# One-core encoder kernel: loads reordered, condition pieces taken three chunks later, two chunks in banks of their own

## The chip, the cores and the metric

The kernel runs on one core of a Trainium2 chip. The metric is device time in microseconds (us) of one execution, the median of several runs. TensorE, VectorE, ScalarE and GpSimd are called PE, DVE, ACT and POOL in the rows; SP is SyncE, which issues every load.

## The reference

It is a chain of transformer blocks on one sequence of 512 positions and width 1024, all in float32. Cut to its steps:

```python
def first_block(x, mem, ...):
    proj = rms_norm(x, g) @ w_in                  # 1024 -> 3080: queries, keys, values, gates
    mix = concat(fox_attention, chunked_rel_attention) @ w_out
    x = x + rms_norm(mix)
    x = x + rms_norm(memory_cross_attention(...)) # w_mem_q, w_mem_kv, w_mem_o, 4 heads
    return x + rms_norm((silu(h @ gate) * (h @ up)) @ w_down)      # 1024 -> 2816 -> 1024

def second_block(x, c, ...):
    ada = silu(c) @ ada_w[l] + ada_b[l]           # 14 groups of 1024 numbers in all
    x = x + g1 * rmsnorm(mlstm_mixer(modulate(rmsnorm(x)), a_w_in, a_w_out))
    x = x + g2 * rmsnorm(square(relu(h @ w1)) @ w2)                # 1024 -> 4096 -> 1024
    ... # layer 2: latent attention (mla), then the same kind of MLP
```

## The kernel before

Everything lies transposed in SBUF: 8 blocks of 128 features by 512 positions. Each float32 product is made of three products of rounded halves: weight and input are split in a high part (rounded, fp32r) and a low part (the rest), and `three` (L774 to L778) issues high x high, high x low, low x high. PE works chunk by chunk: a chunk is 128 output features from one panel of weights (128x1024, 512 KB), 8 x 3 = 24 matmuls of 512 columns.

A panel passes four engines in order. SP loads it into `stage[:, slot]` (two slots, `load_panel`, L538), and may do so once the panel two before it is split (`s_split`). ACT copies it into its high part (`panel_high`, L1372), which it does in `used(p)` (L1390): it waits until PE has finished panel p, then waits for the landing of panel p+2, and copies that. POOL makes the low part (`split_low`, L656) and raises `s_split`, for which PE waits. The first four panels of a projection of the list JOINT have four pairs of weight buffers (EXTRA), so that ACT takes panels 4 and 5 already in `used(0)` and `used(1)`, and nothing in `used(2)` and `used(3)`.

Beside the panels the same SP queue loads 112 "condition pieces" (512 KB each, `load_piece`, L543), rows of the ada weights. Two slots again: piece q may be loaded once DVE has used piece q-2 (`s_pused`). DVE multiplies a piece by the condition vector and sums it into one column (`piece`, L2068). The queue is one list, in order: where SP waits for a piece's slot, the panels behind it wait too. The lists are written out by hand: `start_pieces`, `with_pieces`, `end_pieces` for w_in and a_in (panel, piece, piece, panel, ...), and L618 to L634 for the gated feed-forward.

In the projections w_in (16 chunks, then 8 value panels) and a_in (8 + 8 chunks, then 8 value panels) the chunks alternate between PSUM banks G[0] and G[1]; chunk c waits until DVE has taken chunk c-2 (`bank_free`). ACT's order for chunk c is: `used(c)`, that is the wait for panel c+2 and its copy, and then the copy of the result (L1451). DVE takes the low part of the result (`evacuate_low`, L2162) and then two pieces. After w_in's 16 chunks DVE waits for the gate logits, and ACT computes their logarithm after `used(16)` (L1468 to L1481).

The gated feed-forward has 11 groups of 6 panels: `up(g)` 4 panels (gate and up, twice), `down(g)` 2 panels. PE's order is up(0), up(1), down(0), up(2), down(1), up(3), ... With the panels counted from the stage's first, down(i) has panels 8+6i and 9+6i, up(i+2) has 10+6i to 13+6i. DVE takes four pieces after `add(g)`, the sum of down(g)'s eight results into Y. The two MLPs have the same form without a gate, with 2 + 2 panels per group and banks G[0] and G[1].

Other places of the change: the start (squares of x, their sum over partitions by PE, L883, the root, then the scaled input, L2006 and L2012), the self-attention's products with the values (`weigh`, L953, L979 to L982), the queries of the memory attention (mem_q), and the start of the latent attention (mla). `warm` (L865) issues matmuls whose result nobody reads.

## Time and profile before

| | us |
|---|---|
| median of 3 runs (2259.15 to 2264.13) | 2264.07 |
| the profiled execution | 2257.02 |
| its span | 2255.2 |
| PE busy | 2127.5 (94%) |
| DVE busy | 1087.3 (48%) |
| POOL busy | 958.2 (42%) |
| ACT busy | 876.0 (39%) |

PE is busy for 94% of the span. In the chain that ended last, 72% is PE and 13% "issue". Busy time says nothing of PE's clock: a matmul of 512 columns follows the one before it after 0.23 us at the full clock, and after 0.43 us where the granted clock is half. Rows of the timeline give start, duration, engine, line, operation, tiles, and in brackets the idle time before and what ended it. Rows of the windows view give for a stretch: its length, then busy us and count of PE, PEld, DVE, ACT, POOL, then the granted clock, the DMA share and GB/s.

### The profile page before, as it was taken

To read this page: it belongs to the slowest core of one execution; us is meant where nothing else is said; L and a number is where in the kernel's file an instruction comes from. 1 tells how busy PE (TensorE), PEld (TensorE's weight loads), DVE (VectorE), ACT (ScalarE), POOL (GpSimd) and SP (SyncE) were. 2 spreads that over 40 slices of the span, in tenths; PEclk is the share of its full clock that TensorE was granted. 3 is DMA by queue.
4 is the path that set the end of the run, shared out by engine and by line. 5 is a ranking of instruction groups with operands and counts; after the bars stand their busy time and mean duration, and the time that the engine had idled before them with its cause. 6 is when DMAs were issued, how large, how long until landed. Compare 5 with 4: busy or idle time off the path is not lost.

```text
span 2255.2 us, 27272 instructions
## 1 busy us (share of the span) xinstructions
PE 2127.5 (94%) x9534; PEld 1693.5 (75%) x9534; DVE 1087.3 (48%) x1672; ACT 876.0 (39%) x1442; POOL 958.2 (42%) x489
## 2 busy tenths in 40 slices
PE   5899889889999999889998999999999999999997
PEld 3777678677788888667766688888777776888886
DVE  2753661422465556655364543343565425343435
ACT  4224774344422222424265423222465544232332
POOL 2335676353344444423313344444435533444443
PEclk8999999999999999999999999999998999999999
DMA  4671034112254454347102223323222012233322
GB/s 172 211 266 45 20 116 146 57 37 75 66 179 159 156 171 164 112 159 262 65 1 69 67 84 95 101 93 95 91 78 72 1 47 66 88 98 93 100 95 84
DMA packets 66607, 234.38 MB, mean 104 GB/s; under 512 B 7136, under 2 KB 8416, under 8 KB 66400
## 3 DMA queue, kind: packets, MB, share of 16 engines
q1 hardware_dynamic: 66528, 233.33, 31.7%
q8 instruction: 49, 0.80, 0.1%
q14 instruction: 30, 0.25, 0.0%
HBM read 231.20 MB, written 2.10 MB: 103 GB/s over the span
## 4 chain that ended last, share of the span: by engine, by line
PE 72%; issue 13%; DVE 5%; ACT 5%; POOL 4%; DMA 1%; POOLq 0%; SPq 0%; DVEq 0%; ACTq 0%
PE bank L776 22%; PE bank L777 21%; PE bank L778 21%; POOL WL L658 3%; PE bank L883 2%; PE bank L868 1%; PE bank L950 1%; DVE H L2006 1%; DVE bank L2012 1%; PE bank L1017 1%; DVE Y L2248 0%; ACT Y L1556 0%; PE bank L889 0%; PE bank L1051 0%; PE bank L1276 0%
## 5 line engine op out<-in xcount | busy, mean ns | idle before, releaser
L658 POOL TENSOR_TENSOR WL<-stage,WH 128x1024 fp32r<-128x1024 f32 x272 | 660.6, 2429 | 1028.2 <-ACT WH L1378 1028.1
L1378 ACT ACTIVATE WH<-stage 128x1024 fp32r<-128x1024 f32 x272 | 288.2, 1060 | 918.6 <-PE bank L778 881.0
L776 PE MATMUL bank<-H,WH 128*128 128x512 f32 x1324 | 522.0, 394 | 25.3 <-DVE H L2006 11.8
L777 PE MATMUL bank<-H,WH 128*128 128x512 f32 x1324 | 519.4, 392 | 0.0
L778 PE MATMUL bank<-H,WL 128*128 128x512 f32 x1324 | 518.9, 392 | 0.0
L776 PEld LDWEIGHTS bank<-H,WH 128*128 128x128 f32 x1324 | 250.8, 189 | 84.9 <-issue 30.6
L778 PEld LDWEIGHTS bank<-H,WL 128*128 128x128 f32 x1324 | 250.8, 189 | 52.6
L777 PEld LDWEIGHTS bank<-H,WH 128*128 128x128 f32 x1324 | 250.9, 190 | 52.1 <-issue 0.5
L776 PE MATMUL bank<-HID,WH 128*128 128x512 f32 x688 | 268.8, 391 | 5.4 <-DVE Y L2248 5.4
L2248 DVE TENSOR_TENSOR Y<-bank,Y 128x512 f32<-128x512 f32 x344 | 226.3, 685 | 97.3 <-PE bank L778 96.4
L778 PE MATMUL bank<-HID,WL 128*128 128x512 f32 x688 | 268.4, 390 | 0.0
L777 PE MATMUL bank<-HID,WH 128*128 128x512 f32 x688 | 268.4, 390 | 0.0
L2071 DVE SCALAR_TENSOR_TENSOR apiece<-apiece,cond 128x1024 f32<-128x1024 f32 x112 | 184.9, 1665 | 106.9 <-DMA apiece<-ada 106.7
L2234 DVE SCALAR_TENSOR_TENSOR t<-bank,t 128x512 f32<-128x512 f32 x64 | 44.3, 692 | 276.5 <-ACT t L1599 276.4
L776 PEld LDWEIGHTS bank<-HID,WH 128*128 128x128 f32 x688 | 129.6, 188 | 32.5 <-issue 5.8
L2238 DVE TENSOR_TENSOR HID<-t,HID 128x512 fp32r<-128x512 f32 x86 | 121.3, 1411 | 65.0 <-ACT HID L1604 65.0
L777 PEld LDWEIGHTS bank<-HID,WH 128*128 128x128 f32 x688 | 129.7, 188 | 26.9
L778 PEld LDWEIGHTS bank<-HID,WL 128*128 128x128 f32 x688 | 129.5, 188 | 26.9
L868 PE MATMUL bank<-onesr,identr 128*128 128x512 f32 x284 | 81.8, 426 | 0.0
L690 POOL TENSOR_SCALAR sq<-sq,stat 128x256 f32<-128x256 f32 (+2 forms) x56 | 71.5, 1286 | 19.2 <-DVE stat L2183 19.1
L2177 DVE TENSOR_REDUCE stat<-bank 128x1 f32<-128x128 f32 (+3 forms) x112 | 53.3, 477 | 49.4 <-PE bank L1023 22.6
L1604 ACT ACTIVATE HID<-t 128x512 fp32r<-128x512 f32 x86 | 54.2, 631 | 56.3 <-DVE t L2234 50.6
(394 smaller groups left out, 3075.8 us busy)
## 6 DMA issues: line engine op xcount, KB each, us to landing
stage<-panels SPq DMA_DIRECT2D x296, 512.0 KB, 3.5
apiece<-ada SPq DMA_DIRECT2D x112, 512.0 KB, 4.3
RAW<-panels SPq DMA_DIRECT2D x18, 512.0 KB, 3.8
x<-xT SPq DMA_DIRECT2D x4, 1024.0 KB, 7.8
outT<-x SPq DMA_DIRECT2D x8, 256.0 KB, 2.0
Y<-bias SPq DMA_DIRECT2D x1, 1024.0 KB, 4.8
V<-memT SPq DMA_DIRECT2D x2, 512.0 KB, 4.5
con<-cons SPq DMA_DIRECT2D x1, 517.0 KB, 6.7
```

Of the source, the lines that this page charges most:

```text
L658: pool.tensor_tensor(low_of(p, slot), stage[:, slot, :], high_of(p, slot).bitcast(F32), ALU.subtract).then_inc(s_split, 1)
L690: pool.tensor_scalar(prob[b][:, 0:w], prob[b][:, 0:w], stat[:, 8 + b:9 + b], None, ALU.mult)\
L776: pe.matmul(out, wh, rh, start=start, stop=False)
L777: pe.matmul(out, wh, rl, start=False, stop=False)
L778: return pe.matmul(out, wl, rh, start=False, stop=stop)
L868: pe.matmul(out[:, :], identr[:, :], onesr[:, :].rearrange("p (a b) -> p a b", a=1).to_broadcast([P, 4, P]), start=True, stop=True)
L1378: act.activation(high_of(p, slot), stage[:, slot, :], ACT.Copy).then_inc(s_hisplit, 1)
L1604: act.activation(HID[:, slot, j, 0, :], t[:, j, :], ACT.Copy).then_inc(sm["high"], 1)
L2071: dve.scalar_tensor_tensor(apiece[:, k % 2, :], apiece[:, k % 2, :], 1.0, cond[:], ALU.mult, ALU.mult, accum_out=adac[:, column]).then_inc ...
L2177: dve.tensor_reduce(stat[:, b:b + 1], score_bank[b][:, 0:w], AX, ALU.max, negate=True)\
L2238: dve.tensor_tensor(HID[:, slot, j, 1, :], t[:, j, :], HID[:, slot, j, 0, :].bitcast(F32), ALU.subtract).then_inc(sm["split"], 1)
L2248: dve.tensor_tensor(Y[:, m, :], (T + O)[m % 4][:, :], Y[:, m, :], ALU.add)\
```

## The change

- w_in and a_in: the panels 4 and 5 are loaded ahead of the pieces 2 and 3; then a round of the list is piece, piece, panel, with panel 6 behind the pieces 2 and 3. DVE takes the first two pieces (0 and 1) after chunk 3 and so on, three chunks later than before; the rest follow after the last chunk (w_in: after the gates' first step).
- Chunks 2 and 3 of the JOINT projections go to the banks ST and AD, with no wait for a free bank. The MLPs use four banks in place of two.
- Gated feed-forward: pieces 40 to 43 are taken after `hidden(0)`, and each later four a group earlier. In SP's list the round of six panels with four pieces begins with panel 8 and piece 44, where it began with panel 12 and piece 42.
- Start: x is loaded in three parts, a small part of the constants (ident, ones) second, panels 0 and 1 ahead of the rest; PE waits for ones alone. ACT makes the extra panels after blocks 4 and 6 of the input. The condition's Silu moves behind chunk 0.
- mem_q: four panels are copied earlier, between squares and between blocks of the input.
- Self-attention: a pair's eight value products are spread over seven of eight steps; the results' copies and the values' staging move two steps later. mla: 12 `warm` matmuls ahead of it.

```diff
@@ -36,7 +36,11 @@
+PIECE_LAG = 3
+X_PARTS = [range(0, 2), range(2, 4), range(4, 8)]
+WEIGHED_AT = [[(0, 0), (0, 1)], [(1, 0), (1, 1)], [], [(0, 2)], [(1, 2)], [(0, 3)], [(1, 3)], []]
...
@@ -380,6 +384,10 @@
+        def own_bank(name, c):
+
+            return [ST, AD][c - 2] if name in JOINT and c in (2, 3) else G[c % 2]
...
@@ -530,10 +538,18 @@
         def _(sp):
-            sp.dma_start(x[:, 0:4, :], xT[0:4 * P, :].rearrange("(c p) t -> p c t", p=P)).then_inc(s_x, 16)
-            sp.dma_start(con[:], cons).then_inc(s_const, 16)
-            sp.dma_start(x[:, 4:8, :], xT[4 * P:8 * P, :].rearrange("(c p) t -> p c t", p=P)).then_inc(s_x2, 16)
+            for at, part in enumerate(X_PARTS):
+                sp.dma_start(x[:, part.start:part.stop, :],
+                             xT[part.start * P:part.stop * P, :].rearrange("(c p) t -> p c t", p=P))\
+                    .then_inc(s_x[at], 16)
+                if at == 0:
+                    sp.dma_start(con[:, 0:CON["mask"]], cons[:, 0:CON["mask"]]).then_inc(s_ones, 16)
             sp.dma_start(vec[:], vecs).then_inc(s_const, 16)
+            for slot in range(2):
+                sp.dma_start(stage[:, slot, :], panels[slot]).then_inc(s_stage[slot], 16)
...
@@ -545,29 +561,13 @@
-                        load_panel(i * 4 + (p0 + j), j % 2)
                         load_piece(i * 8 + (q0 + 2 * j), 0)
                         load_piece(i * 8 + (q0 + 2 * j + 1), 1)
-
-            def end_pieces(p0, q0, panels):
-
-                for j in range(max(panels, 3)):
-                    if j < panels:
-                        load_panel(p0 + j, j % 2)
-                    if j < 3:
-                        load_piece(q0 + 2 * j, 0)
-                        load_piece(q0 + 2 * j + 1, 1)
+                        load_panel(i * 4 + (p0 + j), j % 2)
 
@@ -578,13 +578,18 @@
 
-            sp.dma_start(cond[:], c).then_inc(s_c, 16)
-            sp.dma_start(wgate[:], gates_w).then_inc(s_gw, 16)
-            start_pieces(0, 0)
+            load_piece(0, 0, True)
+            load_piece(1, 1, True)
+            plain(2, 4)
             sp.wait_ge(s_h, row(MAKES, "x")[1])
             sp.dma_start(Y[:, 0:4, :].rearrange("p a b -> p (a b)"), bias).then_inc(s_bias, 16)
-            with_pieces(4, 2, 4)
-            end_pieces(20, 34, 6)
+            plain(4, 6)
+            pieces_ahead(6, 2, 4)
+            for j in range(4):
+                if j < 3:
+                    load_piece(34 + 2 * j, 0)
...
@@ -616,28 +621,31 @@
-            plain(p0, p0 + 12)
+            plain(p0, p0 + 4)
             load_piece(q0, 0)
             load_piece(q0 + 1, 1)
-            with sp.Fori(0, 4) as i:
-                for half in range(2):
-                    for j in range(6):
-                        load_panel(i * 12 + (p0 + 12 + 6 * half + j), j % 2)
-                        if j < 4:
-                            load_piece(i * 8 + (q0 + 2 + 4 * half + j), j % 2)
-            for j in range(6):
-                load_panel(p0 + 60 + j, j % 2)
-                if j < 4:
-                    load_piece(q0 + 34 + j, j % 2)
-            load_piece(q0 + 38, 0)
-            load_piece(q0 + 39, 1)
-            plain(p0 + 66, p0 + 68)
+            plain(p0 + 4, p0 + 8)
+            load_piece(q0 + 2, 0)
+            load_piece(q0 + 3, 1)
+            with sp.Fori(0, 9) as i:
+                for j in range(6):
+                    load_panel(i * 6 + (p0 + 8 + j), j % 2)
+                    if j < 4:
+                        load_piece(i * 4 + (q0 + 4 + j), j % 2)
+            plain(p0 + 62, p0 + 68)
             p0, q0 = PANEL0["a_in"], 80
             plain(p0 + 2, p0 + 4)
             load_piece(q0, 0)
             load_piece(q0 + 1, 1)
-            with_pieces(p0 + 4, q0 + 2, 3)
-            end_pieces(p0 + 16, q0 + 26, 8)
+            plain(p0 + 4, p0 + 6)
+            pieces_ahead(p0 + 6, q0 + 2, 3)
+            for k in range(26, 30):
+                load_piece(q0 + k, k % 2)
+            load_panel(p0 + 18, 0)
+            load_piece(q0 + 30, 0)
+            load_piece(q0 + 31, 1)
+            load_panel(p0 + 19, 1)
+            plain(p0 + 20, p0 + 24)
...
@@ -780,10 +788,14 @@
-                bank_free(pe, name, c)
+                if isinstance(c, int) and c in (2, 3) and name in JOINT:
+                    held = own_bank(name, c)
+                else:
+                    bank_free(pe, name, c)
...
@@ -976,10 +988,9 @@
                             score_pair(s + 4)
-                        if s >= 8 and s % 8 < 4:
-                            n, piece = 2 * (s // 8 - 1) + s % 2, s % 8 // 2 * 2
-                            weigh(n, piece)
-                            weigh(n, piece + 1)
+                        if s >= 8:
+                            for h, piece in WEIGHED_AT[s % 8]:
...
@@ -1066,8 +1076,10 @@
-                            if not (isinstance(g, int) and g == 0):
+                            if gated and not (isinstance(g, int) and g == 0):
                                 pe.wait_ge(sm["hidden"], g * 2 + j - 1)
+                            if not gated and not (isinstance(g, int) and g < 2):
...
@@ -1351,6 +1363,7 @@
+            warm(AD, 12)
...
@@ -1570,7 +1583,7 @@
-                        if s >= 12 and s % 8 in (4, 5):
+                        if s >= 12 and s % 8 in (6, 7):
...
@@ -1661,25 +1674,28 @@
-            squares("x", xc, lambda m: act.wait_ge(s_x if m < 4 else s_x2, 16))
+            squares("x", xc, lambda m: [act.wait_ge(s_x[at], 16) for at, part in enumerate(X_PARTS) if part.start == m])
             panel_high(0, 0)
             panel_high(1, 1)
             root("x")
+            act.wait_ge(s_ones, 16)
             act.wait_ge(s_const, 32)
-            extra_high("w_in", 0)
-            high("x", scaled_in, hh, lambda m: col("zero"))
-            extra_high("w_in", 1)
+            for m in range(KC):
+                high_chunk("x", m, scaled_in, hh, lambda m: col("zero"))
+                if m in (4, 6):
...
             def high_near(c):
 
+                if c == 0:
+                    act.wait_ge(s_c, 16)
...
@@ -1730,6 +1746,9 @@
+                if m in (1, 3):
+                    act.wait_ge(s_used, PANEL0["mem_v"] + m // 2 + 1)
+                    panel_high(RING1 + m // 2, m // 2)
...
-            panel_high(RING1, 0)
-            panel_high(RING1 + 1, 1)
             for m in range(KC):
                 high_chunk("x_mem", m, scaled_mem_in, hh, lambda m: col("zero"))
+                if m in (2, 5):
+                    act.wait_ge(s_used, RING1 - 1 + (m - 2) // 3)
+                    extra_high("mem_q", (m - 2) // 3)
             memory_values(1)
-            extra_high("mem_q", 0)
-            extra_high("mem_q", 1)
             evacuate_high("mem_q", lambda c: QKH[:, 8 + c, :], lambda c: 256 ** -0.5)
...
@@ -2250,14 +2274,21 @@
-                hidden(0, 0)
-                with dve.Fori(0, (groups - 1) // 2) as i:
+                def two_groups(i, pieces_then):
                     hidden(i * 2 + 1, 1)
                     add(i * 2)
-                    pieces(i, 0)
+                    pieces(i, range(4, 8))
                     hidden(i * 2 + 2, 0)
                     add(i * 2 + 1)
-                    pieces(i, 1)
+                    if pieces_then:
+                        pieces(i, range(8, 12))
+
+                twice = (groups - 1) // 2
+                hidden(0, 0)
+                pieces(0, range(0, 4))
+                with dve.Fori(0, twice - 1) as i:
+                    two_groups(i, True)
+                two_groups(twice - 1, False)
...
@@ -2298,11 +2330,12 @@
-                for q in (2 * c, 2 * c + 1):
-                    piece(q, 16 * (q // 2 + 1), slice(q, q + 1))
+                if c == 0:
+                    dve.wait_ge(s_cond, 1)
+                if c >= PIECE_LAG:
+                    pieces_of(2 * (c - PIECE_LAG), 2 * (c - PIECE_LAG) + 2)
                 if c == 3:
...
@@ -2318,10 +2351,11 @@
                     last.then_inc(s_sel, 1)
-            add_bias(0, 4)
             dve.wait_ge(s_gl, 2)
             log_gates(0, 0, VEC["b_f"])
             dve.tensor_copy(gs[:], lf[:]).then_inc(s_gate, 1)
+            pieces_of(2 * (16 - PIECE_LAG), 32)
+            add_bias(0, 4)
...
@@ -2369,8 +2403,9 @@
                 evacuate_low("a_in", c, QKH[:, c, :], QKL[:, c, :], 1.0 if c // 4 % 2 else 64 ** -0.5)
-                for q in (80 + 2 * c, 81 + 2 * c):
-                    piece(q, 16 * (q // 2 + 1), slice(q, q + 1))
+                if c >= PIECE_LAG:
+                    pieces_of(80 + 2 * (c - PIECE_LAG), 82 + 2 * (c - PIECE_LAG))
+            pieces_of(96 - 2 * PIECE_LAG, 96)
```

## Rows read from the trace of the kernel before

**Rows 1.** The page's first line.

```profile
span 2255.2 us, 27272 instructions
```

**Rows 2.** Windows view: the w_in stage, and the gated feed-forward.

```profile
29.86:192.10 162.24, 149.58 (x613) 116.52 (x614) 94.28 (x133) 45.61 (x62) 55.18 (x23) 0.94 0.59 201
...
555.00:941.90 386.90, 379.91 (x1644) 308.81 (x1643) 220.58 (x253) 113.58 (x142) 167.42 (x69) 1.00 0.44 144
```

**Rows 3.** Timeline, w_in: from the landing of panel 4 to that of panel 5.

```profile
44.61 1.06 ACT L1378 ACTIVATE WH<-stage 128x1024 fp32r<-128x1024 f32 x1 [1.34 <-DMA stage<-panels]
...
45.74 2.36 POOL L658 TENSOR_TENSOR WL<-stage,WH 128x1024 fp32r<-128x1024 f32 x1 [4.64 <-ACT WH L1378]
46.26 0.69 DVE L2167 SCALAR_TENSOR_TENSOR QKL<-bank,QKH 128x512 fp32r<-128x512 f32 x1 [2.60 <-ACT QKH L1451]
46.86 2.32 DVE L2071 SCALAR_TENSOR_TENSOR apiece<-apiece,cond 128x1024 f32<-128x1024 f32 x1
...
49.11 1.21 DVE L2071 SCALAR_TENSOR_TENSOR apiece<-apiece,cond 128x1024 f32<-128x1024 f32 x1
...
51.03 0.33 SPq L541 DMA_DIRECT2D stage<-panels  x1
...
56.65 1.06 ACT L1378 ACTIVATE WH<-stage 128x1024 fp32r<-128x1024 f32 x1 [10.50 <-DMA stage<-panels]
```

**Rows 4.** Timeline of ACT, a_in: panels 4, 5 and 21 copied.

```profile
969.31 1.06 ACT L1378 ACTIVATE WH<-stage 128x1024 fp32r<-128x1024 f32 x1 [2.68 <-PE bank L778]
...
980.75 1.06 ACT L1378 ACTIVATE WH<-stage 128x1024 fp32r<-128x1024 f32 x1 [9.90 <-DMA stage<-panels]
...
1087.51 1.06 ACT L1378 ACTIVATE WH<-stage 128x1024 fp32r<-128x1024 f32 x1 [4.97 <-PE bank L778]
```

**Rows 5.** Timeline of SP's queue, a_in: two panel loads, eight rounds apart.

```profile
1020.56 0.33 SPq L541 DMA_DIRECT2D stage<-panels  x1
...
1068.35 5.64 SPq L541 DMA_DIRECT2D stage<-panels  x2
```

**Rows 6.** Timeline, feed-forward: first and second chunk of an up, piece, piece load.

```profile
660.01 0.39 PE L776 MATMUL bank<-H,WH 128*128 128x512 f32 x1
...
660.82 1.22 DVE L2071 SCALAR_TENSOR_TENSOR apiece<-apiece,cond 128x1024 f32<-128x1024 f32 x1
...
662.22 0.33 SPq L546 DMA_DIRECT2D apiece<-ada  x1
...
665.45 0.39 PE L776 MATMUL bank<-H,WH 128*128 128x512 f32 x1
```

**Rows 7.** Panel loads (L541) in 560 to 930 us: from issue to landing.

```profile
DMA to landing us min/median/max: 3.4/3.5/5.2
```

**Rows 8.** Windows view: two stretches at half the granted clock.

```profile
47.80:51.20 3.40, 3.40 (x9) 2.67 (x9) 2.53 (x4) 0.00 (x0) 0.30 (x1) 0.50 0.18 30
...
1734.00:1754.50 20.50, 20.50 (x59) 15.08 (x60) 4.30 (x14) 4.83 (x16) 6.86 (x7) 0.50 0.00 1
```

**Rows 9.** Timeline: the start of the kernel.

```profile
11.06 9.46 PE L883 MATMUL bank<-sq,con 128*128 128x512 f32 x14 [11.06 <-DMA vec<-vecs]
...
23.59 1.41 DVE L2012 SCALAR_TENSOR_TENSOR bank<-x,vec,bank 128x512 f32<-128x512 f32 x2 [22.70 <-ACT bank L1424]
...
27.29 1.06 ACT L1378 ACTIVATE WX<-stage 128x1024 fp32r<-128x1024 f32 x1 [3.81 <-DMA stage<-panels]
...
29.86 0.76 PE L776 MATMUL bank<-H,WH 128*128 128x512 f32 x1 [8.29 <-DVE H L2006]
```

**Rows 10.** Timeline of PE: waits in mem_q, at the feed-forward's end, in the first MLP.

```profile
432.27 0.76 PE L776 MATMUL bank<-H,WZ 128*128 128x512 f32 x1 [7.33 <-DVE QKL L2167]
...
932.15 0.76 PE L776 MATMUL bank<-HID,WH 128*128 128x512 f32 x1 [5.42 <-DVE Y L2248]
...
1282.66 0.47 PE L776 MATMUL bank<-H,WX 128*128 128x512 f32 x1 [2.80 <-DVE t L2234]
```

**Rows 11.** Waits of PE, whole span: us in total, times, longest.

```profile
PE bank L776 <- DVE QKL L2167: 32.2, 11, 7.3
...
PE bank L950 <- POOL sq L690: 9.7, 9, 1.6
```

More of the change, by code:

```diff
@@ L1055, in feed_forward @@
                 sm = ff[name]
-                banks = [G[0], G[1], ST, AD] if gated else [G[0], None, G[1], None]
                 per = 2 if gated else 1
@@ L1060, in up @@
                     p = ff_up(name, g)
+                    banks = [G[0], G[1], ST, AD] if gated else [(G[0], ST)[slot], None, (G[1], AD)[slot], None]
                     if isinstance(g, int) and g == 0:
@@ L1589, in feed_forward @@
                 sm = ff[name]
-                banks = [G[0], None, ST, None] if gated else [G[0], None, G[1], None]
                 per = 2 if gated else 1
@@ L1594, in through @@
                     p = ff_up(name, g)
+                    banks = [G[0], None, ST, None] if gated else [(G[0], ST)[slot], None, (G[1], AD)[slot], None]
                     for j in range(2):
@@ L2072, in piece, with pieces_of @@
                                          ALU.mult, accum_out=adac[:, column]).then_inc(s_pused, 1)
+            def pieces_of(first, last):
+                for q in range(first, last):
+                    piece(q, 16 * (q // 2 + 1), slice(q, q + 1))
             def add_bias(g0, n):
```

65 lines of the change are left out of this document (34 added, 31 removed).

## Prediction

> **What bounds the kernel now.** I read the page first: TensorE is busy for 2127.5 of 2255.2 us [rows 1], so only a change of what TensorE waits for, or of its clock, can move the end. Then the windows of the stages the change touches: in w_in TensorE is busy for 149.6 of 162.2 us at a mean granted clock of 0.94, in the gated feed-forward for 379.9 of 386.9 us at the full clock [rows 2]; there the panels come in time and little can be won. Then the waits of TensorE: 32.2 us in 11 waits on VectorE's low copies of projection results, 9.7 us on the scaled probabilities in the attentions [rows 11]. Last, the timelines around these waits, to see what VectorE, ScalarE and the load queue had waited for in turn. A chunk is 24 matmuls; the two chunks of the feed-forward begin at 660.01 and 665.45, so it lasts 5.44 us [rows 6].
>
> **The loop that the new order closes (w_in).** One long stall of before shows its mechanism whole [rows 3]. At 44.61 panel 4 has landed and ScalarE copies it; then the result of chunk 0 is copied, VectorE takes its low part (46.26) and piece 0 (46.86), which ends only at 49.11, since GpSimd's split runs from 45.74 to 48.10; then piece 1 (1.21). Only now may SP load the next two pieces, and behind them panel 5 (51.03), which lands at 56.65. Landing to landing is 12.04 us. In a_in the same takes 980.75 - 969.31 = 11.44 us [rows 4]; mean 11.7.
>
> Before, that happens once per stage: panel 5 hangs on VectorE's chunk 0 and is wanted in `used(1)`, one chunk on. From there panel p hangs on the pieces of chunk p-5 and is wanted in `used(p-2)`: three chunks of slack, and 12 us fit into 16.3. The change frees panels 4 and 5, but moves the rest. Panel 6 now stands behind piece 3, whose slot is free when piece 1 is used, that is with chunk 3. In general panel p waits for the pieces of chunk p-3, and ScalarE wants it in `used(p-2)`, ahead of copying chunk p-2, on which VectorE's next pieces wait. So the stall of [rows 3] recurs for every panel from 6 on, at 11.7 us where TensorE needs 5.44. Not even an instant landing would save it: from the copy at 44.61 to the panel's issue at 51.03 it is 6.4 us.
>
> The w_in sum, in us from the span's start. The sum of squares no longer waits for all constants (it began at 11.06), and ScalarE no longer waits 3.81 for panel 2 ahead of the input [rows 9]. The first bytes needed are about 0.66 MB in place of 2.8 MB; I put the start of the sum 5 us earlier, which with the 3.8 makes 8.9, and the projection starts at 21 instead of 29.86 (bounds 0 and 10 us; near the upper, as both waits stand in the rows). Four chunks of 5.44 plus 2 for the low clock at the start: chunk 3 ends at 45. Panel 6 lands after the two copies (1.3), two pieces (2 x 1.2), 0.7 to issue and 5.6 to land, 9.9 in all: at 54.9. Panel 18 lands 12 turns of 11.7 later, at 195. ScalarE takes it in `used(16)`, and only behind it the gates' logarithm; VectorE then goes on with piece 26, so panel 19 lands another 11.7 later, 207. From there pieces run free: in a_in eight such rounds took 1068.35 - 1020.56 = 47.8, or 6.0 each [rows 5]. Panel 21 lands at 219; its copy (1.06) and four result copies (about 0.6 each) end at 222.5; four value panels of 5.44 end at 244. Before the stage ended at 191.9: **+52** (38 if a turn costs 10.6, with no lock; 65 if TensorE, idle half of the time, enters the tail at the low clock).
>
> That GpSimd's split holds up the piece is in the Trainium skill too (SBUF — State Buffer, Who interferes with whom): a DVE instruction with two SBUF inputs contends with a GpSimd one that reads SBUF. By that rule, with the 2.32 against 1.21 us of [rows 3] agreeing, each turn keeps its 1.1 us of lock; where the order of issue changed so that VectorE came first, the page would let GpSimd wait instead, and the sum would be about the same, since the panel needs both.
>
> **a_in.** Same lists, 8 chunks with pieces. Pair start unchanged; panels 4 and 5 come early, chunk 3 ends near 980.6, panel 6 lands at 990.5, panel 10 four turns later at 1037. Then pieces 90 to 111 run free at 6.0 a round, eleven rounds, to about 1102. ScalarE takes the logarithm of the gates, which waits for them, ahead of panel 19: split 3.5 later and computed by 1111. Before, ScalarE saw that chunk's end at 1087.51 [rows 4]: **+23** (10 to 35: how many rounds at 11.7, and whether the free rounds take 5.5 or 6.5).
>
> **Gated feed-forward.** SP's round is now P8, p44, P9, p45, P10, p46, P11, p47, P12, P13. Piece 46 needs piece 44 used, which follows add(0), that is the end of down(0); behind it stands P11, the second chunk of up(2). Before, the first panel held like that was P13, two chunks later. In [rows 6] down ends at 660.01, the first piece runs at 660.82, its successor is issued at 662.22. P11 would be issued 0.5 later, at 662.7, land in 4.3 (between the 3.5 and 5.2 of [rows 7], since a piece is ahead of it), be copied in 1.06 and split in 2.4 [rows 3]: ready at 670.6, wanted at 665.45. That is 5.1 of idle TensorE for each of nine rounds (3.6 to 6). After such waits the clock falls: the wait of 4.1 us that ended at 47.09 was followed by 3.4 us at half clock [rows 8], which costs 1.7 (0 to 3.4). So 9 x 6.8 = 61 (33 to 85). The pieces that delayed the last group are gone with their wait of 5.42 [rows 10] and a low stretch, -7. Together **+54**. The cover that is lost is the two panels' lead; nothing else hides it, since TensorE had no slack there [rows 2].
>
> The Trainium skill (TensorE: Matmul & The Clock Gate, HAM oscillation) describes loops that wait for a DMA in each turn and start each turn cold. It agrees with [rows 8]; by its rule every one of the nine rounds pays the 1.7, without it the sum is 15 less.
>
> **The gains elsewhere.** mem_q: the wait of 7.33 [rows 10] and half-speed time behind it go, less what two more copies among the inputs' cost: -10 (-7 to -11). The MLPs: 2.80 [rows 10] and a low stretch each, twice: -9 (-5 to -9); TensorE doesn't wait inside them, so the extra banks bring nothing more. mla: 20.5 us at half clock [rows 8]; the 12 warm matmuls fill a wait and may hold the clock: -7 (+2 to -10). Self-attention: some waits of the 9.7 [rows 11] may be filled by the moved products, but the results leave their banks two steps later: -3 (-8 to +4). The first stall of a_in is within its sum.
>
> **Sum.** +52 +54 +23 -10 -9 -7 -3 = +100 on the profiled execution, 2257, gives 2357. That execution is 7 us under the median of the runs, 2264; the other way of counting gives 2364. I say 2360.
>
> **Rivals.** (1) The reverse, faster: SP's waits don't hold the panels. The mechanism would be that VectorE gets through its pieces ahead of the panel it hangs on, and it decides at 5.44 us a turn; then w_in gains 29 (8.9 at the start, some 12 of waits, 8 of low clock), a_in 13, the feed-forward 7, the rest 29: -78, or 2180. Against it are the 6.4 us of serial work in [rows 3] and the two stalls of before with the same members. 5%. (2) Only the feed-forward doesn't stall, because P11 comes by 662, for instance as DMA and copies run shorter than now: +39, 2300. Against it [rows 7]'s minimum of 3.4: even then it is 4 us late. 6%. (3) The loops hold and the small gains fail, as the warm matmuls and later results cost what they bring: +129, 2388. 12%. (4) The clock stays low for two stretches in each round and in the projections' tails: 15 more in the feed-forward, 25 in the projections, 2400. 13%. The forecast, 64%, between 2335 and 2385.
>
> **Range and chances.** The bounds of the terms together would reach from about 2300 to 2425; leaving out case 1 and the ends, 2305 to 2412. A measurement tells about 0.3% (7 us) from no change. Slower 0.94, same 0.01, faster 0.05.
>
> **What would show it.** In w_in and a_in ScalarE's copies of panels 6 to 18 (6 to 10) wait for the DMA and follow each other at 11 to 12 us, SP waits long for VectorE's pieces, and TensorE waits for GpSimd's split. In the feed-forward nine waits of about 5 us before the second chunk of an up, and a granted clock that dips behind them. The first projection starts near 21. If the copies follow each other at 5.5 us, the loop is wrong and the time falls; if they do at 8 or 9, the turn is mis-sized.

## The result, and the profile after

The changed kernel takes 2363.02 us (median of 4 runs, 2359.3 to 2368.88), the kernel before 2261.61 in the runs beside it (2254.16 to 2264.13). The ratio is 1.0456, with a 95% interval of 1.0422 to 1.0491: 101 us slower. The forecast was 2360. The profiled execution of the changed kernel took 2362.48 us, its span 2360.7.

First the page of the changed kernel: the span, the busy times, the chain that ended last, and from the costliest groups the first of the three products of a chunk (L784).

```profile
span 2360.7 us, 27273 instructions
...
PE 2162.7 (92%) x9546; PEld 1713.9 (73%) x9546; DVE 1086.5 (46%) x1672; ACT 875.8 (37%) x1442; POOL 955.3 (40%) x489
...
PE 55%; issue 28%; POOL 8%; DVE 4%; ACT 4%; DMA 1%; POOLq 0%; DVEq 0%; ACTq 0%; SPq 0%
...
L784 PE MATMUL bank<-H,WH 128*128 128x512 f32 x1324 | 544.6, 411 | 127.1 <-POOL WL L666 118.7
```

VectorE, ScalarE and GpSimd have the same work to do as before. TensorE is busy 35 us longer, with 12 matmuls more, and idle 70 us longer. In the chain, "issue" has gone from 13% to 28%. The last column of the matmul row names what TensorE waits for now: the low part of a weight panel, which GpSimd makes.

The waits of TensorE over the whole span, of the changed kernel (us in total, times, longest; L2190 and L962 are L2167 and L950 of before):

```profile
PE bank L784 <- POOL WL L666: 133.5, 32, 6.8
...
PE bank L962 <- POOL sq L698: 6.4, 9, 1.6
...
PE bank L784 <- DVE QKL L2190: 4.7, 2, 2.4
```

The 32.2 us on the low copies of [rows 11] are down to 4.7. What has come in their place, four times as large, is the first line, the wait for the low part of a weight panel. In the kernel before it was small:

```profile
PE bank L776 <- POOL WL L658: 5.1, 3, 3.0
```

What stands behind it is in the waits of the load queue, of the changed kernel and then of the kernel before:

```profile
SPq L562 <- DVE apiece L2089: 426.2, 80, 23.1
```

```profile
SPq L546 <- DVE apiece L2071: 223.1, 87, 15.8
```

SyncE stands 426 us in front of condition pieces whose slot VectorE has not freed, twice as long as before, and whatever panels are behind them in its list stand too. The total alone doesn't measure the loss: before, with 223 us of such waits, ScalarE waited some 10 us for such a panel once in w_in and once in a_in ([rows 3], [rows 4]). What counts is which panel stands behind the piece, and when it is wanted.

Where the time lies shows in a table by stage. Each length is between the starts of the same matmul in the two traces; the third column is of the kernel e4, told of below.

| stage | before | after | e4 | after - before |
|---|---|---|---|---|
| start, to the first projection | 29.86 | 20.20 | 20.14 | -9.7 |
| w_in | 162.04 | 228.11 | 156.43 | +66.1 |
| self-attention | 126.62 | 117.72 | 117.96 | -8.9 |
| memory keys to mem_q | 151.21 | 142.69 | 142.70 | -8.5 |
| memory attention | 85.38 | 85.10 | 86.62 | -0.3 |
| gated feed-forward | 385.88 | 447.23 | 378.60 | +61.3 |
| a_in and the cells | 197.37 | 223.49 | 191.10 | +26.1 |
| a_out | 112.61 | 113.30 | 113.37 | +0.7 |
| first MLP | 372.36 | 367.68 | 367.69 | -4.7 |
| mla: inputs | 61.62 | 60.57 | 60.63 | -1.1 |
| mla: attention and output | 183.54 | 172.55 | 172.50 | -11.0 |
| second MLP | 372.37 | 367.68 | 367.69 | -4.7 |

The windows view, with the same columns as [rows 2], for the w_in stage and the gated feed-forward of the changed kernel:

```profile
20.20:248.31 228.11, 168.95 (x612) 128.98 (x613) 96.77 (x133) 45.97 (x62) 54.77 (x23) 0.84 0.43 146
...
593.82:1041.05 447.23, 400.44 (x1641) 321.42 (x1640) 215.59 (x249) 112.45 (x142) 165.66 (x69) 0.94 0.36 124
```

and of the kernel before, between the same matmuls:

```profile
29.86:191.90 162.04, 149.38 (x613) 116.33 (x614) 94.28 (x133) 45.61 (x61) 55.18 (x23) 0.94 0.59 201
...
555.11:940.99 385.88, 378.89 (x1642) 308.29 (x1640) 219.82 (x249) 112.61 (x142) 167.38 (x69) 1.00 0.44 143
```

They split the loss. In w_in TensorE is idle for 228.11 - 168.95 = 59.2 us where it was 12.7 (+46.5), and busy 19.6 us longer with the same matmuls, since the clock fell from 0.94 to 0.84; with the start's -9.7 that is +56.4. In the feed-forward idleness goes from 7.0 to 46.8 (+39.8) and busy time up by 21.6, at a clock of 0.94 in place of 1.00.

One turn of the w_in loop, in the timeline of the changed kernel, from the landing of panel 6 to that of panel 7, and at the end the landings of panels 17 and 18:

```profile
54.00 1.06 ACT L1391 ACTIVATE WH<-stage 128x1024 fp32r<-128x1024 f32 x1 [9.03 <-DMA stage<-panels]
...
55.14 2.34 POOL L666 TENSOR_TENSOR WL<-stage,WH 128x1024 fp32r<-128x1024 f32 x1 [11.20 <-ACT WH L1391]
55.58 0.69 DVE L2190 SCALAR_TENSOR_TENSOR QKL<-bank,QKH 128x512 fp32r<-128x512 f32 x1 [5.39 <-ACT QKH L1464]
56.18 2.38 DVE L2089 SCALAR_TENSOR_TENSOR apiece<-apiece,cond 128x1024 f32<-128x1024 f32 x1
...
58.49 1.21 DVE L2089 SCALAR_TENSOR_TENSOR apiece<-apiece,cond 128x1024 f32<-128x1024 f32 x1
...
60.41 0.33 SPq L557 DMA_DIRECT2D stage<-panels  x1
...
66.42 1.06 ACT L1391 ACTIVATE WH<-stage 128x1024 fp32r<-128x1024 f32 x1 [10.88 <-DMA stage<-panels]
...
187.03 1.06 ACT L1391 ACTIVATE WH<-stage 128x1024 fp32r<-128x1024 f32 x1 [10.46 <-DMA stage<-panels]
...
198.86 1.06 ACT L1391 ACTIVATE WH<-stage 128x1024 fp32r<-128x1024 f32 x1 [9.82 <-DMA stage<-panels]
```

It is the picture of [rows 3], member for member, but now it recurs: in brackets ScalarE waits 7.7 to 11.4 us for the DMA ahead of each copy. From 54.00 to 198.86 twelve turns take 144.9 us, 12.07 each.

And one round of the feed-forward, changed kernel: the piece that SyncE waits for, its successor's load (L562), the panel behind it (L557), the landing, the split, and TensorE's wait; below it the last of the nine.

```profile
666.88 1.22 DVE L2089 SCALAR_TENSOR_TENSOR apiece<-apiece,cond 128x1024 f32<-128x1024 f32 x1
...
668.28 0.33 SPq L562 DMA_DIRECT2D apiece<-ada  x1
668.80 0.33 SPq L557 DMA_DIRECT2D stage<-panels  x1
...
673.31 1.06 ACT L1391 ACTIVATE WH<-stage 128x1024 fp32r<-128x1024 f32 x1 [11.41 <-DMA stage<-panels]
...
674.44 2.34 POOL L666 TENSOR_TENSOR WL<-stage,WH 128x1024 fp32r<-128x1024 f32 x1 [10.06 <-ACT WH L1391]
...
676.83 0.80 PE L784 MATMUL bank<-H,WH 128*128 128x512 f32 x1 [5.16 <-POOL WL L666]
...
998.32 0.80 PE L784 MATMUL bank<-H,WH 128*128 128x512 f32 x1 [4.95 <-POOL WL L666]
```

There are nine such waits, of 4.93 to 5.16 us, 45.3 in all.

### The profile page after: what moved, and what is told of

It is laid out like the page before. It is cut to its first block, busy times and chain, and to the rows that moved or that the text cites. A ratio compares the mean times of both kernels' runs of the same rounds, so it can differ in the third digit from the quotient of the medians.

```text
span 2360.7 us, 27273 instructions
## 1 busy us (share of the span) xinstructions
PE 2162.7 (92%) x9546; PEld 1713.9 (73%) x9546; DVE 1086.5 (46%) x1672; ACT 875.8 (37%) x1442; POOL 955.3 (40%) x489
## 4 chain that ended last, share of the span: by engine, by line
PE 55%; issue 28%; POOL 8%; DVE 4%; ACT 4%; DMA 1%; POOLq 0%; DVEq 0%; ACTq 0%; SPq 0%
PE bank L784 16%; PE bank L785 16%; PE bank L786 16%; POOL WL L666 6%; PE bank L895 2%; PE bank L880 1%; PE bank L962 1%; POOL sq L698 1%; POOL t L698 0%; DVE acc L2000 0%; DVE Y L2272 0%; DVE bank L2073 0%; PE bank L1288 0%; ACT sq L1419 0%; PE bank L1027 0%
## 5 line engine op out<-in xcount | busy, mean ns | idle before, releaser
L784 PE MATMUL bank<-H,WH 128*128 128x512 f32 x1324 | 544.6, 411 | 127.1 <-POOL WL L666 118.7
L785 PE MATMUL bank<-H,WH 128*128 128x512 f32 x1324 | 537.0, 406 | 0.0
L786 PE MATMUL bank<-H,WL 128*128 128x512 f32 x1324 | 534.7, 404 | 0.0
L784 PEld LDWEIGHTS bank<-H,WH 128*128 128x128 f32 x1324 | 262.3, 198 | 198.1 <-POOL WL L666 91.1
L786 PEld LDWEIGHTS bank<-H,WL 128*128 128x128 f32 x1324 | 261.7, 198 | 57.9
L785 PEld LDWEIGHTS bank<-H,WH 128*128 128x128 f32 x1324 | 262.9, 199 | 55.4 <-issue 0.5
L784 PE MATMUL bank<-HID,WH 128*128 128x512 f32 x688 | 267.6, 389 | 0.0
L784 PEld LDWEIGHTS bank<-HID,WH 128*128 128x128 f32 x688 | 129.1, 188 | 26.8
L2190 DVE SCALAR_TENSOR_TENSOR QKL<-bank,QKH 128x512 fp32r<-128x512 f32 x40 | 27.3, 690 | 181.5 <-ACT QKH L1464 178.0
L2256 DVE TENSOR_TENSOR t<-bank,t 128x512 f32<-128x512 f32 x22 | 15.2, 691 | 135.7 <-PE bank L786 135.5
```

What stands on the lines that cost most here:

```text
L784: pe.matmul(out, wh, rh, start=start, stop=False)
L785: pe.matmul(out, wh, rl, start=False, stop=False)
L786: return pe.matmul(out, wl, rh, start=False, stop=stop)
```

## The experiments

Two theories of the loss stood against each other. The loop: a panel hangs on a piece that VectorE takes late, and the loss depends on how many chunks lie between the chunk whose pieces it hangs on and the chunk that wants it. The queue: 1 MB of pieces ahead of each panel, or pieces among the panels at all, make the panels late, wherever VectorE takes them. Twelve kernels were run. A ratio is to the kernel before, with its 95% interval. The kernels e1 to e4 and e9 to e11 are edits of the changed kernel; e5 to e8 and e12 are edits of e4.

**e1, the pieces one chunk late.**

```diff
-PIECE_LAG = 3
+PIECE_LAG = 1
```

> The changed kernel with PIECE_LAG = 1 in place of 3: VectorE takes the pieces of chunk c-1 with chunk c, so panel p hangs on the pieces of chunk p-5 again; the order of the load queue (two pieces ahead of each panel) and all else stay. Theory (the turn of 12.07 us is a loop over one chunk; over three chunks it would be 4.0 us per chunk, under TensorE's 5.44): from panel 6 on TensorE doesn't wait, w_in ends 29 us earlier than in the kernel before and a_in 13 earlier, in place of 56.4 and 26.1 later; so 2363 - 85 - 39 = 2239 us, and ScalarE's copies of panels 7 to 18 follow each other at 5.4 to 5.6 us. Rival (the order of the queue itself makes each panel late, since 1 MB of pieces goes ahead of it, or the transfers take the turn's 12 us): the lag makes little difference, 2340 to 2363 us, copies at 10 us or more.

Measured: 2258.95 us, ratio 1.0002 (0.9990 to 1.0014), 104 us under the changed kernel. One number is changed, the order of the queue is not, and the whole loss of w_in and a_in goes: w_in takes 155.1 us from its first product, a_in and the cells 190.3. The queue theory (2340 to 2363) falls. The time is 20 us above what the loop theory gave, though. ScalarE's copies in this kernel:

```profile
53.48 1.06 ACT L1391 ACTIVATE WH<-stage 128x1024 fp32r<-128x1024 f32 x1 [9.93 <-PE bank L786]
58.92 1.06 ACT L1391 ACTIVATE WH<-stage 128x1024 fp32r<-128x1024 f32 x1 [3.89 <-PE bank L786]
...
121.52 1.06 ACT L1391 ACTIVATE WH<-stage 128x1024 fp32r<-128x1024 f32 x1 [4.15 <-PE bank L786]
132.50 1.06 ACT L1391 ACTIVATE WH<-stage 128x1024 fp32r<-128x1024 f32 x1 [4.85 <-PE bank L786]
```

They now wait for TensorE, not for the DMA, as in the kernel before. I had counted all waits and low clock of w_in and a_in as gone, and they are not. The timeline of e1 shows one that stays:

```profile
42.96 0.60 ACT L1464 ACTIVATE QKH<-bank 128x512 fp32r<-128x512 f32 x1 [1.25 <-PE bank L786]
...
44.22 1.22 DVE L2089 SCALAR_TENSOR_TENSOR apiece<-apiece,cond 128x1024 f32<-128x1024 f32 x1
...
45.37 0.68 DVE L2190 SCALAR_TENSOR_TENSOR QKL<-bank,QKH 128x512 fp32r<-128x512 f32 x1
...
46.10 0.50 PE L784 MATMUL bank<-H,WH 128*128 128x512 f32 x1 [3.18 <-DVE QKL L2190]
```

The low part of a result stands behind two pieces on VectorE, and TensorE waits for its bank. 12.9 us of such waits are in e1, 7.7 of them in w_in. So w_in and the start together gain 17.5 us over the kernel before, not 29, and a_in 7, not 13; those two make up 17.5 of the 20.

**e2, two chunks late.** `PIECE_LAG = 2`.

> The same with PIECE_LAG = 2: panel p hangs on the pieces of chunk p-4. Theory: the same serial turn of 12.07 us then spans two chunks, 6.03 per panel against 5.44, so 13 panels of w_in cost some 7 us over the lag of 1 and those of a_in 3: 2249 us, copies of panels at 6.0 us on the mean. Rival (the loss goes up in proportion to the lag, each chunk of lag making the panels later): halfway between the lags of 1 and 3, about 2300 us, copies at 9 us.

Measured: 2263.14 us, ratio 1.0019 (1.0000 to 1.0037), w_in 157.0 us, a_in and the cells 193.1. With 1, 2 and 3 chunks of lag w_in takes 155.1, 157.0 and 228.1 us. That isn't in proportion, so the rival falls; the corner lies between a slack of two chunks (lag 2) and of one (lag 3). The copies in e2:

```profile
52.51 1.06 ACT L1391 ACTIVATE WH<-stage 128x1024 fp32r<-128x1024 f32 x1 [8.37 <-DMA stage<-panels]
58.51 1.06 ACT L1391 ACTIVATE WH<-stage 128x1024 fp32r<-128x1024 f32 x1 [4.46 <-DMA stage<-panels]
...
130.15 1.06 ACT L1391 ACTIVATE WH<-stage 128x1024 fp32r<-128x1024 f32 x1 [4.81 <-PE bank L786]
```

The first two follow at 6.0 us, and all copies from panel 6 to panel 17 are released by the DMA, so the loop does set the pace here, as the theory has it. But the twelve steps from panel 6 to panel 18 take 77.6 us, 6.47 each, a turn of 12.9 us over two chunks, and in e1, where TensorE and not the loop releases the copies, they take 79.0. There TensorE has the gates' 24 matmuls to do among the chunks (one step of 11.0 us) and waits of 2.1 and 2.4 us for its banks, so that its own mean pace is some 6.5 us, not 5.44 (6.42 in the kernel before, 77.0 for the same twelve). A loop that takes as long over two chunks costs nearly nothing against that (4 us in the medians, where I had put 10).

**e3, the feed-forward's pieces one panel later.**

```diff
-                    if j < 4:
-                        load_piece(i * 4 + (q0 + 4 + j), j % 2)
+                    if 1 <= j < 5:
+                        load_piece(i * 4 + (q0 + 3 + j), (j - 1) % 2)
```

> The changed kernel with the four piece loads of each feed-forward round put one panel later in the load queue (P8, P9, p44, P10, p45, P11, p46, P12, p47, P13); the projections stay as changed. Theory: now P12 stands behind piece 46, it is ready at the same time after the end of the down (10.6 us on), and is wanted 10.9 us on: the nine waits of 4.9 to 5.2 us and the low clock behind them go, 61.4 + 7 less, or a little more than 0 stays of each: 2295 to 2303 us. Rival (the stall is the price of four pieces among six panels, wherever they stand): the nine waits move one chunk later and stay at 4 to 5 us, 2350 to 2363 us.

Measured: 2297.22 us, ratio 1.0157 (1.0134 to 1.0179), 66 less. The stage takes 379.2 us in place of 447.2, and no wait above 0.3 us is left among its groups. Same pieces, same number of them between the panels: it is their place that costs, by one panel. Piece 46 now holds P12, wanted 10.9 us after the end of the down, and that is enough.

**e4, both.** `PIECE_LAG = 1`, and the pieces of the feed-forward two panels later (`2 <= j < 6`).

> PIECE_LAG = 1 and the feed-forward's piece loads two panels later, all other parts of the change kept. Theory: no turn is closed in under three chunks any more, and what is left are the parts that gain (from the profiles after: self-attention 8.9, mem_q 8.5, MLPs 8.6, mla 12.0) and what the early start brings to w_in (29) and the list to a_in (13) and the feed-forward (7): 2262 - 87 = 2175 us. Rival (the gains of the other stages are borrowed from the stalls, for instance from transfers that the longer stages leave time for): 2200 to 2240 us.

Measured: 2189.14 us (2182.97 to 2191.59), ratio 0.9685 (0.9669 to 0.9702): 3.1% faster than the kernel before and the fastest of those with all of the work, together with e12, which can't be told from it. The 14 us over the expectation are in w_in and a_in, as in e1, since I had put the same 29 and 13 there. The stages (third column of the table) are those of the changed kernel where they gained, so their gains were not borrowed from the stalls. Its waits:

```profile
PE bank L784 <- POOL WL L666: 13.7, 7, 4.6
PE bank L784 <- DVE QKL L2190: 13.5, 7, 2.5
```

The next five put one small part of the change back in e4, for the terms that I had only estimated.

**e5, the self-attention's products as before.** The products' place in the loop is the hunk below; the steps at which the results are copied, the values staged and the squares added go back with it:

```diff
-                        if s >= 8:
-                            for h, piece in WEIGHED_AT[s % 8]:
-                                weigh(2 * (s // 8 - 1) + h, piece)
+                        if s >= 8 and s % 8 < 4:
+                            n, piece = 2 * (s // 8 - 1) + s % 2, s % 8 // 2 * 2
+                            weigh(n, piece)
+                            weigh(n, piece + 1)
```

> The kernel with PIECE_LAG = 1 and the later piece loads (2189 us), and in it only the self-attention's products put back in their order of before (both halves of a pair's products within four steps, results copied at steps 4 and 5). Theory: the 8.7 us that this stage is shorter than in the kernel before are all of the spread products: +8.7, 2198 us, with a wait of 2.1 us on VectorE's PT back in the stage. Rival (my prediction's sum of 3 us was right for the products and the rest came with the stage's start, whose waits and clock depend on what TensorE did just before): +3, 2192 us.

Measured: 2200.64 us, ratio 0.9750 (0.9722 to 0.9779), 11.5 more. The windows view of e5 for this stage, and then that of e4:

```profile
174.98:302.52 127.54, 107.66 (x701) 85.11 (x700) 78.14 (x220) 88.19 (x247) 89.30 (x75) 0.92 0.07 26
```

```profile
176.57:294.53 117.96, 105.96 (x701) 83.45 (x700) 75.52 (x220) 87.96 (x247) 88.58 (x75) 0.94 0.08 28
```

The spreading brings 9.6 us in these two profiles: idle time goes from 19.9 to 12.0, busy time down by 1.7 with the clock. The size is not better known than by a few us, since in the twelve profiles with the spread products the stage takes 112.0 to 118.6 us, with and without stretches at half clock. e4's is among the long ones. The rival (3 us) falls all the same. In e5 fifteen waits of 0.8 to 2.2 us on GpSimd's scaled probabilities and on VectorE's PT stand in the stage besides the one on the norm; with the products between them six above 0.6 are left.

**e6, without the warm matmuls ahead of the latent attention.** `warm(AD, 12)` taken out.

> The same kernel of 2189 us without the 12 warm matmuls ahead of the latent attention. Theory: they alone made the stage shorter (11 to 12 us from the sum of one residual to that of the next): 20.5 us at half clock come back, +11, 2200 us, and the wait of 2.4 us at the attention's start with them. Rival (the warm matmuls take the time of the wait that they fill and bring 2 us or less, and the gain came from another part of the stage): +2 or less, 2189 to 2191 us.

Measured: 2196.93 us, ratio 0.9721 (0.9691 to 0.9751), 7.8 more in the medians and 10.3 in the stage (182.80 against 172.50 us). The same 25 us of e6, and then of e4, windows view:

```profile
1680.00:1705.00 25.00, 22.60 (x71) 16.35 (x69) 7.77 (x20) 7.07 (x20) 7.44 (x7) 0.59 0.05 18
```

```profile
1680.00:1705.00 25.00, 25.00 (x133) 19.20 (x131) 11.48 (x31) 10.93 (x33) 11.77 (x11) 1.00 0.03 12
```

Without them a wait of 2.40 us is back, and the granted clock is half for 20.5 us behind its end, as in [rows 8]:

```profile
1683.12 0.30 PE L784 MATMUL bank<-QKH 128*128 128x128 f32 x1 [2.40 <-DVE ROT L2557]
```

With them TensorE is at 1.00 throughout and gets through 133 matmuls (12 of them the warm ones) instead of 71. The 10.3 us of the stage are an upper value: with the warm matmuls in place it takes 172.5 to 173.1 us in six profiles, e4's among them, but 175.3 to 175.6 in six others (e1, e2, e3, e5, e11, e12). Later in the stage the clock falls once more in e4, twice more in e6, and at least twice in five of those six. Against those the matmuls bring 7.3, near the 7.8 of the medians.

**e7, the MLPs on two banks.** `[(G[0], ST)[slot], None, (G[1], AD)[slot], None]` back to `[G[0], None, G[1], None]`, on all three engines.

> The same kernel of 2189 us with the MLPs on two banks (G[0], G[1]) again. Theory: each MLP gets its one wait of 2.8 us back before its second group, with a stretch at the low clock behind it of 1.9: +9.3, 2198 us. Rival (the four banks also carry waits inside the loop that the profile of before hides as it shows none over 0.5 us): more than 12. That the banks bring nothing: 2189 us.

Measured: 2196.86 us, ratio 0.9726 (0.9692 to 0.9759), 7.7 more. Each MLP takes 372.38 us in place of 367.68, 4.7 for each, with the one wait back:

```profile
1232.84 0.47 PE L784 MATMUL bank<-H,WX 128*128 128x512 f32 x1 [2.78 <-DVE t L2256]
```

**e8, chunks 2 and 3 of mem_q in the alternating banks.** `own_bank` with `name != "mem_q"`.

> The same kernel of 2189 us with chunks 2 and 3 of the memory attention's query projection in the two alternating banks again; ScalarE's copies of the panels stay among the input's. Theory (the banks remove the wait of 7.33 us and the half clock behind it, whatever the copies do): +8.5, 2198 us. Rival (the copies, taken earlier, let ScalarE reach the results in time, and the banks add nothing): 2189 to 2191 us, with a wait on VectorE's low part of under 2 us.

Measured: 2192.74 us, ratio 0.9702 (0.9674 to 0.9731). The stage takes 144.78 us against 142.70, with this wait:

```profile
404.07 0.47 PE L784 MATMUL bank<-H,WZ 128*128 128x512 f32 x1 [1.85 <-DVE QKL L2190]
```

That is 2.1 of the 8.5 us (3.6 in the medians), and the rival held for the most part: the earlier copies alone bring most of it.

**e12, the same copies back in their place, the banks kept.**

```diff
-                if m in (2, 5):
-                    act.wait_ge(s_used, RING1 - 1 + (m - 2) // 3)
-                    extra_high("mem_q", (m - 2) // 3)
             memory_values(1)
+            extra_high("mem_q", 0)
+            extra_high("mem_q", 1)
```

and likewise for the two copies among the squares.

> The kernel of 2189 us with the banks of its own for chunks 2 and 3 kept, and ScalarE's four copies of the memory stage's weight panels put back to where they were (two ahead of the root, two behind the whole input and the memory values). Putting the banks back alone lengthened the stage from 142.7 to 144.8 us, by 2.1 of the 8.5 that the change takes from it. Theory (the two edits add up, and the copies carry the rest): +6.4, the stage 149.1 us, 2196 us, a wait of about 4 us in the query projection. Rival (either edit alone takes most of the wait of 7.3): +2 at most, 144 to 145 us, 2191 us.

Measured: 2187.86 us, ratio 0.9683 (0.9662 to 0.9704), the stage 142.82 us. The theory of e12 is wrong, its rival right: the two edits don't add up. The banks alone bring the whole 8.5, the copies alone 6.4, and the longest wait left in the stage, 1.1 us on GpSimd's low part of a panel, doesn't lengthen it.

**e9, the waits of the feed-forward filled.** In the changed kernel:

```diff
+                            if name == "ffn" and q == 1 and not (isinstance(g, int) and g < 2):
+                                pe.wait_ge(sm["hidden"], g * 2 + j - 1)
+                                warm(banks[1], 21)
                             pe.wait_ge(s_split, p + (q + 1))
```

> The changed kernel (2363 us), in which TensorE fills each of the nine waits in the gated feed-forward with 21 warm matmuls of 512 columns (4.8 us at the full clock, nobody reads them) into the bank that its next chunk will overwrite. The waits themselves stay. Theory (the 61 us of this stage are 45.5 of waiting and, behind each wait, 2.7 to 6.1 us at half clock, 42 us in all, which cost 21): with the filling the clock stays, 21 less, 2342 us, and no stretch at half clock in the stage. Rival (the low clock behind a wait is no matter of TensorE's idleness, or it falls all the same): 2358 to 2368 us, stretches at half clock as before.

Measured: 2341.61 us, ratio 1.0372 (1.0352 to 1.0393), 21.4 less, as the theory has it. The stage in e9, windows view:

```profile
593.73:1020.79 427.06, 422.80 (x1830) 341.82 (x1829) 213.54 (x249) 112.51 (x142) 165.06 (x69) 1.00 0.38 130
```

The granted clock is 1.00, and the time of the nine waits is still spent, now on the warm matmuls: a round takes 38.1 us (from 790.66 to 828.77), 5.4 more than the 32.64 that six panels take without a wait. So of the 61 us of this stage about 20 are clock and the rest is waiting. It is no way to make the kernel fast: it repays a third of a loss that e3 avoids.

**e10, half the work of a piece.** In `piece`, the columns 0 to 511 of both inputs in place of all.

> The changed kernel, in which VectorE multiplies and sums only the first 512 of the 1024 columns of each condition piece (half of the condition sums is left out); the loads stay whole. It measures VectorE's part of the turn of 12.07 us. Theory (VectorE's first piece waits for the end of GpSimd's split, then runs at its own pace): the first takes 2.4 - 0.6 = 1.8 us, the second 0.6, the turn is 1.2 shorter, 10.9, and w_in 14 us, all 2338 to 2342 us. Rival on the piece (both run at once, each slower): the first takes 1.2, the turn is 1.8 shorter, 10.3, 2328 to 2332 us. Rival on the loop (the turn is the time of the transfers): 12 us as before, 2360 us.

Measured: 2327.43 us, ratio 1.0305 (1.0259 to 1.0351), from two runs 15 us apart (2319.72 and 2335.14). A turn of e10:

```profile
52.62 2.37 POOL L666 TENSOR_TENSOR WL<-stage,WH 128x1024 fp32r<-128x1024 f32 x1 [9.45 <-ACT WH L1391]
...
53.67 1.87 DVE L2089 SCALAR_TENSOR_TENSOR apiece<-apiece,cond 128x512 f32<-128x512 f32 x1
...
55.47 0.68 DVE L2089 SCALAR_TENSOR_TENSOR apiece<-apiece,cond 128x512 f32<-128x512 f32 x1
```

The second piece falls from 1.21 to 0.68 us, the first only from 2.38 to 1.87: GpSimd's split ends at 54.99, and 0.55 later the piece is done. That is the first theory of the piece, and it speaks against the two running side by side. From 51.49 to 179.90 the copies of panels 6 to 18 take 128.4 us, 10.70 a turn, so VectorE's work is on the turn, and the loop isn't made of transfers alone. All is 36 us faster, where 21 to 25 were expected; that total would fit the rival on the piece (2328 to 2332) better. Against the rival stand the piece itself and the turn, 10.70 where the theory has 10.9 and the rival 10.3. The total holds more than the turn. By the profiled executions, 43 us apart, w_in ends 20.3 earlier, not 14: the turn is 1.37 shorter rather than 1.2 (12 x 1.37 = 16.4), and the rest lies ahead of panel 6 and in the rounds behind panel 18. The self-attention is 5.7 us shorter, with no piece in it, and has no stretch at half clock in e10. The feed-forward is 6.1 us shorter, a_in with the cells 11.0; why these two gain as they do was not pursued.

**e11, and half the load too.**

```diff
-                sp.dma_start(apiece[:, slot, :], ada[q]).then_inc(s_piece[slot], 16)
+                sp.dma_start(apiece[:, slot, 0:S], ada[q][:, 0:S]).then_inc(s_piece[slot], 16)
```

> As the last, and the piece loads too fetch only the first 512 columns (256 KB in place of 512). It measures what the two transfers ahead of a panel cost. Theory: a panel then lands some 3.7 us after its issue in place of 5.2, so the turn is 1.5 shorter again, 9.4 us, still above the 5.44 that TensorE needs, and w_in still waits in each chunk; some 2313 us. Rival (the transfers are the turn): half the bytes of the pieces bring it to 8 us or less, 2300 us or less.

Measured: 2302.64 us, ratio 1.0195 (1.0169 to 1.0222), from two runs. The edit of VectorE's work of e10 is in it too. Issue to landing of a panel, e11:

```profile
68.14 0.33 SPq L557 DMA_DIRECT2D stage<-panels  x1
...
72.93 1.06 ACT L1391 ACTIVATE WH<-stage 128x1024 fp32r<-128x1024 f32 x1 [6.80 <-DMA stage<-panels]
```

It is 4.8 us where e10 has 5.5 (67.62 to 73.09) and I expected 3.7; over the panels of this loop the medians are 4.6 and 5.3. The turn is 10.03 us, 0.67 shorter, not 1.5. Neither number that I gave for the turn was met (9.4, or 8 and less), and the time lies between the two that I gave (2313, or 2300 and less). With half the bytes ahead of it a panel saves 0.7 us, and the turn stays near twice TensorE's 5.44. Halving both the pieces' arithmetic and their bytes takes 2.0 of 12.07 us; the rest is the chain of copies, low part, split, issue and the panel's own landing, which runs once per turn, in series.

## Why the prediction was right, point by point

- **The start**, -8.9: measured -9.7. TensorE's first product now waits 4.6 us for GpSimd's low part of the weights instead of the input, which I hadn't named. It isn't the transfers: the first two panels land at 11.3 and 12.6 us (13.9 and 16.4 before). ScalarE copies them only after the last of the eight squares, from 14.3, and GpSimd's two splits then run until 20.1.
- **The turn of w_in**, 11.7: measured 12.07. Panel 6 was put at 54.9 and landed at 54.00, panel 18 at 195 and landed at 198.86: the twelve turns are 12 x 0.37 = 4.4 us longer than in the sum, and 0.9 was to spare. Panels 19 and 21 landed at 211.26 and 223.36 against 207 and 219, 12.4 and then 6.05 a round, as forecast. The stage ended at 248.31 against 244: **+56.4 for +52**. The mis-sized term is the turn, taken as a mean of the two stalls of before.
- **The clock in w_in** isn't in my sum, and needn't be. TensorE was busy 19.6 us longer, but in a loop that it waits for, slower matmuls only shorten the wait. That only holds where the loop doesn't pass through TensorE; its members above are all of other engines, and the turn at a clock of 0.84 (12.07) is that of the single stall of before (12.04). No run changed the clock in w_in alone. The dearer case of my range, a tail at the low clock, didn't come: the last copies, from 232.19 to 243.07, follow at 5.44 us.
- **a_in**, +23: measured **+26.1**. Panel 6 landed 32.5 us after the stage's start (forecast 31.7), and four turns took 12.04 each.
- **The feed-forward**, +54: measured **+61.3**. The nine waits are 5.1 us as worked out, from 4.93 to 5.16. The low clock behind them is the mis-sized part: I gave each 1.7 us from the 3.4 us of [rows 8]; the nine stretches in which matmuls follow each other at 0.43 us last 2.7 to 6.1 us, some 43 in all, which costs 21, 2.4 each. e9 took 20 to 21 of them away. The gain that I set against them, 7, came: without the nine waits the stage is 7.3 shorter than before (e4). The Trainium skill (TensorE: Matmul & The Clock Gate, HAM oscillation) describes a loop that waits in each turn and starts each one cold; the trace agrees in that all nine rounds do.
- **mem_q**, -10: measured -8.5. e8 and e12 say what I had left open: either edit alone would have brought most of it.
- **The MLPs**, -9: -9.4, and e7 shows it is the banks, by the one wait at each MLP's start.
- **mla**, -7: measured -12.0, outside my bounds (+2 to -10), of which the warm matmuls carry 7.3 to 10.3 (e6). I had been too careful: the stretch at half clock in [rows 8] is 20.5 us long, so it costs some 10, and in e4 it is gone whole. Later in the stage the clock falls twice in the kernel before and once in the changed one, which is in the 12.0 too.
- **Self-attention**, -3: measured -8.9, just outside my bounds (-8 to +4); e5 gives 9.6 to the spreading, with the scatter told of there. The step that failed is the cover. I took the later results as a cost and counted only GpSimd's waits of [rows 11], 9.7 us; those on VectorE's PT, 6.7 us in e5, were not in it. In e4 the first kind is down from 8.7 to 5.4 us in this stage, the second to 2.1.

The losses come to 56.4 + 26.1 + 61.3 = 143.8 us where I had 129, the gains of the four small parts to 38.8 where I had 29. The two misses, 15 one way and 10 the other, cancel for the most part: +105.5 on the spans for +100. That the total is 3 us off is luckier than the steps are.

The first rival gave 2180 us to the kernel without a loop, and e4, which is that kernel, takes 2189. In the changed kernel its case did not come about: the panels are held, as SyncE's 426.2 us and the twelve turns show. Its sum holds better than its split, for w_in with the start gives 15.3 and not 29, a_in 6.3 and not 13, and the small parts more, which again is luck.

## What to carry to other kernels

When work is deferred, count the slack in units of the consumer's steps: from the step that frees a slot in an in-order queue to the step that wants what stands behind it. A serial turn of 12 us costs nearly nothing over two or three steps of 5.4 to 6.5 us, and 66 us in one stage over a single step. Changing a lag by one (e2), or the place of a load by one panel (e3), is the cheapest fix, and worth trying before a change of many parts is given up: here the lag of 1 and loads two panels later turned +4.6% into -3.1% (e4).

## What the runs showed of the hardware

- A VectorE instruction with two SBUF inputs that meets a GpSimd subtraction waits for its end rather than running at half speed beside it: with half the columns it takes 1.87 us in place of 2.38, and alone 0.68 in place of 1.21 (e10). The Trainium skill (SBUF — State Buffer, Who interferes with whom) says so, an exclusive hold rather than a sharing; the runs agree.
- Waits of nearly the same length (4.93 to 5.16 us) were followed by stretches at half clock of 2.7 to 6.1 us. One such wait is no measure of the next; over nine the mean was 4.8 us. Matmuls that nobody reads, issued in the wait, kept the granted clock at 1.00 in both places where they were tried (e4 against e6, and e9).
- A 512 KB panel behind two pieces landed 5.3 us after its issue (e10, median of the twelve in the w_in loop), and 4.6 with the pieces halved (e11): halving what goes ahead of a transfer took 0.7 to 0.8 us off it.
- The same work can meet the half clock in one kernel and not in another: the self-attention stage, with the same products, took 112.0 us without such a stretch (e10) and 118.0 with 13.6 us of them (e4).
